# First block's attention: the copies of turned probabilities move from VectorE to ScalarE

## The reference

```python
o_a = dsa_attention(...)            # A: softmax over the 64 keys that an indexer scores highest
o_b = forgetting_attention(...)     # B: logits + cumulated log of the forget gates
o_c = differential_attention(...)   # C: softmax(q1 k1) - lam * softmax(q2 k2), then a norm per head
o_d = sliding_window_sink_attention(...)  # D: window of 128 keys, a sink in the denominator
x = x + rmsnorm(concat(o_a, o_b, o_c, o_d) @ w_out, g_post_mix)
```

## Time and profile before

| | us |
|---|---|
| median of 3 runs | 1958.08 |
| lowest, highest | 1957.68, 1962.58 |
| profiled execution | 1962.05 |
| its span, first to last instruction | 1960.2 |
| TensorE matmul busy | 1887.3 (96%) |
| VectorE busy | 1169.7 (60%) |
| ScalarE busy | 885.6 (45%) |

### The profile page before, as it was taken

How to read it: one execution, slowest core, us unless ns; L and a number is a source line. 1 busy time by engine, 2 the same in 40 slices (tenths; PEclk the granted TensorE clock), 3 DMA queues, 4 the chain that set the end, 5 groups by cost and what they waited for, 6 DMA issues and landing times.

```text
span 1960.2 us, 23117 instructions
## 1 busy us (share of the span) xinstructions
PE 1887.3 (96%) x9135; PEld 1553.6 (79%) x9135; DVE 1169.7 (60%) x1360; ACT 885.6 (45%) x1071; POOL 92.6 (5%) x108
## 2 busy tenths in 40 slices
PE   7989999999899999999999999998999999999997
PEld 5877888878778888888877778886888877778885
DVE  5785555657765557456576574556456576574555
ACT  5544444655354435444345443443444345443442
POOL 6310000021200000000000000000000000000000
PEclk9988999999899999999999999999999999999998
DMA  8414655543765555663555645556663556645552
GB/s 254 146 46 133 193 184 169 204 162 124 105 203 193 183 172 213 204 216 100 166 172 199 219 150 181 184 185 210 207 215 98 169 169 208 211 151 183 184 187 89
DMA packets 194385, 340.17 MB, mean 174 GB/s; under 512 B 9342, under 2 KB 59422, under 8 KB 194304
## 3 DMA queue, kind: packets, MB, share of 16 engines
q1 hardware_dynamic: 189072, 327.76, 51.0%
q0 software_dynamic: 5232, 11.29, 3.2%
HBM read 333.24 MB, written 5.77 MB: 173 GB/s over the span
## 4 chain that ended last, share of the span: by engine, by line
PE 86%; DVE 7%; ACT 3%; DVEq 2%; issue 1%; DMA 0%; SPq 0%; ACTq 0%
PE G L647 19%; PE G L648 19%; PE G L652 18%; PE T L700 5%; PE A L647 4%; PE A L648 4%; PE A L652 4%; PE G L662 2%; PE G L663 2%; PE G L668 2%; PE A L759 1%; DVE wlo L1606 1%; PE T L749 1%; PE A L662 1%; ACT whi L1154 1%
## 5 line engine op out<-in xcount | busy, mean ns | idle before, releaser
L1606 DVE TENSOR_TENSOR wlo<-raw,whi 128x2048 fp32r<-128x2048 f32 (+3 forms) x300 | 630.3, 2103 | 570.3 <-ACT whi L1154 570.1
L1154 ACT ACTIVATE whi<-raw 128x2048 fp32r<-128x2048 f32 (+3 forms) x300 | 527.1, 1759 | 587.8 <-PE G L652 512.9
L647 PE MATMUL G<-whi,XH 128*128 128x512 f32 (+1 forms) x1408 | 560.4, 398 | 7.6 <-DVE XL L1620 6.3
L648 PE MATMUL G<-whi,XL 128*128 128x512 f32 (+1 forms) x1408 | 549.6, 390 | 0.0
L652 PE MATMUL G<-wlo,XH 128*128 128x512 f32 (+1 forms) x1408 | 346.2, 388 | 0.0
L647 PEld LDWEIGHTS G<-whi,XH 128*128 128x128 f32 x1408 | 266.1, 189 | 64.3 <-DVE XL L1620 8.0
L648 PEld LDWEIGHTS G<-whi,XL 128*128 128x128 f32 x1408 | 266.3, 189 | 53.8 <-issue 1.9
L652 PEld LDWEIGHTS G<-wlo,XH 128*128 128x128 f32 x1408 | 264.0, 188 | 53.6
L700 PE MATMUL T<-ident,arena 128*128 128x128 f32 x804 | 114.8, 282 | 19.6 <-ACT arena L1154 10.9
L700 PEld LDWEIGHTS T<-ident,arena 128*128 128x128 f32 x804 | 94.6, 144 | 38.2 <-issue 11.8
L1154 ACT ACTIVATE arena<-T 128x512 f32<-128x512 f32 (+2 forms) x92 | 45.9, 549 | 157.5 <-PE T L700 157.4
(11 more groups left out here) (237 smaller groups left out, 2236.9 us busy)
## 6 DMA issues: line engine op xcount, KB each, us to landing
raw<-in_w_in SPq DMA_DIRECT2D x112, 1024.0 KB, 7.3
raw<-in_w_mlp_up SPq DMA_DIRECT2D x32, 1024.0 KB, 5.3
raw<-in_w_mlp_down SPq DMA_DIRECT2D x32, 1024.0 KB, 5.0
raw<-in_w_ffn_gate SPq DMA_DIRECT2D x44, 512.0 KB, 4.1
raw<-in_w_ffn_up SPq DMA_DIRECT2D x44, 512.0 KB, 5.1
raw<-in_w_ffn_down SPq DMA_DIRECT2D x44, 512.0 KB, 3.7
raw<-in_w_out SPq DMA_DIRECT2D x16, 1024.0 KB, 4.9
raw<-in_w_ret_proj SPq DMA_DIRECT2D x16, 1024.0 KB, 5.0
```

The source lines that it names most:

```text
L647: nc.tensor.matmul(dst(m), hx[:, k0 + k, rows], hi[:, k, :], start=first and k == 0, stop=False)
L648: nc.tensor.matmul(dst(m), lx[:, k0 + k, rows], hi[:, k, :], start=False, stop=False)
L1154: return nc.scalar.activation(out_, in_, func, **kw)
L1606: tt(lo_, raw[:, slot, 0:n], hi.bitcast(F32), ALU.subtract).then_inc(part_sem(blk, c, s_lo, s_lo1), 1)
```

## The change

In the first block's attention the copies of `T` to `PT` are taken out of VectorE's loop and written into ScalarE's. In round q ScalarE makes the exponentials of job q, in round 2 then the copies of C's turns and `project`, then the copies of job q - 1, and behind them what rounds 0, 3 (weight splits) and 5 (copies of D's turns) have besides. A round is added at the end for job 9's copies. In rounds with no exponentials left only the copies are made. VectorE's loop is the same without its copies. Number, size and semaphores of the copies stay; the second block has its own functions for this and isn't changed.

```diff
+            def job_copies(L, q):
+                for kt in range(JOBS1[q][1] + 1):
+                    t = T_JOB + job_banks(JOBS1, q) + kt
+                    act.wait_ge(s_t.sem, s_t.at(0, L, t + 1))
+                    act_(PT[:, q % 2, kt], T[:, t % 2, :], ACT.Copy).then_inc(s_tfree.sem, 1)
+
...
-                for q in range(len(JOBS1)):
-                    exps(0, L, q, JOBS1, PR)
+                for q in range(len(JOBS1) + 1):
+                    if q < len(JOBS1):
+                        exps(0, L, q, JOBS1, PR)
                     if q == Q_TURN_C + 1:
                         turn_copy(0, L, T_JOB + job_banks(JOBS1, Q_TURN_C) - 2, 4, QT[:, 13:17])
                         project(0, 6, LAST1)
-                    elif q == Q_TURN_D:
+                    if q:
+                        job_copies(L, q - 1)
+                    if q == Q_TURN_D:
                         turn_copy(0, L, T_JOB + job_banks(JOBS1, Q_TURN_D) - 2, 4, QT[:, 17:21])
                     elif q in (0, 3):
                         hi(0, L, 0, U_OUT + (q == 3))
...
-            def copy_turned(blk, L, q, jobs, t0, dst):
-
-                kind, m, _ = jobs[q]
-                w = 4 * P
-                for kt in range(m + 1):
-                    t = t0 + job_banks(jobs, q) + kt
-                    dve.wait_ge(s_t.sem, s_t.at(blk, L, t + 1))
-                    nc.vector.tensor_copy(dst[:, q % 2, kt, 0:w], T[:, t % 2, 0:w]).then_inc(s_tfree.sem, 1)
-
...
-            def run_jobs(blk, L, jobs, t0, dst, beside=None):
+            def run_jobs(blk, L, jobs, beside=None):
                 for q in range(len(jobs) + 2):
                     if q < len(jobs):
                         prep(blk, L, q, jobs)
                     if q == Q_TURN_C + 1:
 
                         lo(blk, L, 0, U_OUT)
-                    if 1 <= q <= len(jobs):
-                        copy_turned(blk, L, q - 1, jobs, t0, dst)
                     if q >= 2:
                         outputs(blk, L, q - 2, jobs)
...
-                run_jobs(0, L, JOBS1, T_JOB, PT, beside)
+                run_jobs(0, L, JOBS1, beside)
```

## The result

The changed kernel takes 1966.07 us, the median of 20 runs (1958.64 to 1971.74). The kernel before took 1960.54 us beside it on the same chip (20 runs, 1956.17 to 1968.58). The ratio is 1.0024, with a 95% interval from 1.0013 to 1.0035: slower by some 5 us. The time lies inside the forecast's range. The difference is a little under the 0.3% that the forecast had named as its bound, so the branch that it held to be likelier, slower by more than that (0.55), did not come. A later comparison of the same two kernels gave 1.0021 [1.0006, 1.0036].

What follows compares the result with a forecast made beforehand. TensorE, busy for 96% of the span, was taken to bound the kernel. Layer 0 +2.1 and layer 1 2.6 + 2.1 = +4.7 sum to +6.8 us; on 1958.08 that is 1964.9, taken as 1965.3, range 1959.5 to 1969.5.

Steps and rivals of the forecast that it cites:

- Up to job 5's maxima: about 0: Attention jobs before job 5's maxima: these maxima stay where they are, though exponentials 4 come some 0.4 us later.
- D's turns: +1.34 us, hole of 2.6 us: TensorE's turns of D's queries and keys wait for job 4's copies behind exponentials 5: hole grows from 1.70 us.
- After D's turns at full clock: +0.85 us: From D's turns to the jobs' end, clock up: most of 1.34 us made up, 0.85 us left per layer.
- The two terms: At job 7, full clock: maxima and exponentials 0.3 us late, then turn 7 waits 0.5 us for job 6's copies.
- At half clock: +2.1 us: After D's turns with the clock down: 1.34 us goes through whole, plus bank waits; bounds 1.3 and 3.4.
- rival (c): Slower still: slow stretch after D's turns merges with the later one, about 2 us more per layer, 1969; chance 0.11.
- The clock: a first fall in both layers: Half clock behind the 2.6 us hole ahead of D's turns: layer 0 had it (+2.1), layer 1 new (+4.7).
- Base and total: Sum of +6.8 us on the three runs' median 1958.08 gives 1964.9, or 1967.5 on the other base; 1965.3 taken.
- The forecast's own range: Range of the main forecast without rivals, with 1.3 to 3.4 us per layer and base open upwards: 1963.3 to 1968.5.
- Rival (b): Faster: VectorE's relief brings maxima 5 earlier, hole ahead of D's turns shrinks, no fall in layer 0, 1954; chance 0.04.

Runs made afterwards that it cites:

- the second trace: Profile of the changed kernel measured once more, unaltered: 1966.22 us, ratio 1.0021 to the kernel before.
- the first trace: First profiled execution of the changed kernel, unaltered: 1969.56 us, span 1967.8 us.
- the two filled kernels: Kernel before and changed kernel, each with unread matmuls in the holes ahead of D's turns and job 9's turn: ratios 0.9966 and 0.9968.
- the second experiment: Changed kernel with ten extra unread matmuls in the hole ahead of D's turns: 1964.02 us, ratio 0.9993 to the kernel before.
- first experiment: Changed kernel with job 4's two copies moved ahead of the exponentials of job 5: 1956.75 us, ratio 0.9967 to the kernel before.
- fifth: Changed kernel with ScalarE's second output weight split moved from round 3 to the end of round 5: 1969.43 us, ratio 1.0025.
- changed kernel with fills: Changed kernel with ten unread matmuls ahead of D's turns and seven ahead of job 9's turn: 1958.05 us, ratio 0.9968.
- third experiments: Kernel before with six extra unread matmuls in its hole ahead of D's turns: 1958.99 us, ratio 0.9979.
- experiment 10: Kernel before with six unread matmuls ahead of D's turns and seven ahead of job 9's turn: 1955.12 us, ratio 0.9966.
- experiment 7: Changed kernel, job 4's copies ahead of exponentials 5, second weight split at round 5's end, seven unread matmuls ahead of job 9's turn: 1953.04 us, ratio 0.9951.

## Why the prediction was right

**Up to job 5's maxima: about 0.** Held. Maxima 5 came at 120.46 us against 120.58; counted from the first job's maxima they are 0.2 us (layer 0) and 0.3 us (layer 1) later, a term of half a microsecond in all that the sum didn't have. Exponentials 4 were to be 0.4 us late, and were: 20.10 us behind the first job's maxima against 19.68.

**D's turns: +1.34 us, hole of 2.6 us.** Held: 123.24 us forecast as 123.38, and counted from maxima 5 2.78 us against 1.46, +1.32; hole 2.71 and, in the second trace, 2.71 and 2.70 us, released by a ScalarE copy. Only in layer 1 of the first trace it was 1.20, behind the early fall.

**After D's turns at full clock: +0.85 us.** Held: 0.85 us at job 9's maxima between the two filled kernels and 0.82 by the second experiment, both at full clock; at the last output it was 0.71. The two terms as the prediction writes them, 0.3 and 0.5, make 0.8 and not 0.85. The bank wait at turn 7 was set at 0.5 us and measured at 0.64 - 0.06 = 0.58.

**At half clock: +2.1 us.** Held in the second trace of the changed kernel: layer 0, 32.94 - 30.67 = +2.3. In the first it was +3.8, above the upper bound of 3.4, because the clock stayed down for 13.7 us instead of 10.3. The forecast had the place of the fall, not how long it would last, and had put such a merging of slow stretches only into rival (c).

**The clock: a first fall in both layers.** This is the step that carried most of the sum, and the one least safe. The count was right in both traces. The cause, "the hole is longer than 1.92 us", is supported by what removes it: with the hole gone (first experiment) or filled (second, layer 0) there is no first fall, with the hole at 3.2 us (fifth) it is there in both layers. But the hole isn't the only thing that brings the clock down here. In the first trace's layer 1, and in three of the experiments, it fell ahead of D's turns, in the light matmuls of the jobs before; in three of these four cases right at job 4's turn, at a wait of 0.65 or 0.75 us, in the fourth with no wait of more than 0.50 us in the ten microseconds before. The forecast's picture, holes in order of length with a bound somewhere between 1.33 and 1.92 us, fails on both sides: a wait of 1.40 us was followed by a fall (changed kernel with fills, layer 0), and one of 1.92 us was not (first trace, layer 1). What else decides, no run here shows. With the sizes of the second trace the sum would have been +2.3 + 5.0 = +7.3 us, where the forecast had +6.8.

The Trainium skill's rule on pauses ("TensorE: Matmul & The Clock Gate", § A second HAM failure mode: psum-queue depth-cycling), that short pauses between groups of matmuls make the clock swing, fits part of what the traces show: pauses of 1.70 and 2.71 us between groups of matmuls were followed by half clock, and with matmuls in them they were not (layer 0 of the second and third experiments). It was weighed against the step as if it said that a longer pause adds nothing, and the runs speak against that reading: with 2.7 us the fall was there in both layers of the second trace, with 1.70 us in one of two.

**Base and total.** The forecast added 6.8 us to 1958.08 and 0.4 us for the doubt about the base. In the paired runs the difference of the medians is 1966.07 - 1960.54 = 5.5 us, 1.3 us less than the sum, while the base was 2.5 us higher than the three runs had it. That the time came within 0.8 us of the 1965.3 owes something to luck, since these two errors offset each other. The forecast's own range is also added up wrongly: its terms lead from 1963.3 to 1964.9 + 2.6 + 2.6 = 1970.1, where it has 1968.5; the result lies in both.

The likely reason for the smaller difference is that the kernel before has more falls in some of its runs than in its trace. In the five comparisons its median lay between 1960.54 and 1964.77 us, and of the 105 runs of it beside the experiments 27 took over 1967 us, at a mean granted clock of 0.981 or 0.982, as the slowest of the changed kernel; the 11 under 1957 us had 0.989 or 0.990. So the kernel before reaches the slow times too. What the changed kernel hardly has are the fast ones: 1 of its 32 runs was under 1960 us, against 29 of those 105. Where the kernel before's clock fell in them isn't shown, since no trace was taken of such a run.

Rival (b), slower turning to faster because VectorE is relieved, has nothing behind it. ScalarE as such wasn't the problem either: the same copies on it, job 4's in front, are 0.33% faster than before. How much of that is clock, and how much the engine and the order, shows with both holes covered: VectorE's copies reach 0.9966 (experiment 10), ScalarE's in the better order 0.9951 (experiment 7). The 0.15% between them is what engine and order would be worth, with intervals that overlap. The stretch of layer 0, at full clock in both traces, is clearer: 23.93 against 25.83 us, 1.9 us for the engine, the order and the late split together.

What stays open is why the clock fell early in layer 1 in some executions and not in others with the same waits. That job 4's copies alone go back to VectorE wasn't tried: two engines would then signal the same semaphore in no fixed order.

## What to carry to other kernels

When a step moves to an idle engine, look at what stands in front of it in that engine's written order and at who waits for it. Here two copies behind four exponentials cost a hole of 1 us more, and the same two in front of them gave it all back. A hole on the engine that bounds the kernel costs up to its length and, if the clock falls behind it, more in the work that follows (here 2.6 us behind a hole of 1.70); so a hole's price is to be read with the granted clock of the stretch behind it. A hole that can't be closed can be filled with matmuls whose results nobody reads, as here; it didn't keep out the falls that began elsewhere.

## What the runs showed of the hardware

- Useless work made the kernel faster: six matmuls in one hole of each layer 0.9979, thirteen in two holes 0.9966, in the kernel before, otherwise unaltered.
- The granted clock fell to 0.50 at a wait of only 0.65 us, amid turns and outputs of 64 columns, and stayed there for 17.1 us in the first trace of the changed kernel and for 6.8 us in the second experiment, while the same wait in the changed kernel's second trace did nothing. A wait of 1.92 us was followed by a fall in both layers of the kernel before and by none in layer 1 of that first trace. The length of a wait alone doesn't tell.
- Behind a fall TensorE looks fully busy (10.20 of 10.20 us in the second trace of the changed kernel) and does 49 matmuls where at full clock, in the kernel with the hole filled, 80 ran in 10.00 us with 8.97 busy. A busy share of 100% is here the mark of the slow stretch, not of a good one.
- Two copies in a row on ScalarE took 1.09 us where a single one took 0.60 to 0.65: the second costs 0.45 to 0.5 us.
